# A modulation quad moved into the attention jobs, and the first expert's rows made by one-hot products

## The chip, the cores and the metric

The kernel runs on one core of one Trainium2 chip. The metric is the device time of one launch in microseconds (us), the median of several runs. The core has TensorE (PE; its weight loads are listed apart, as PEld), VectorE (DVE), ScalarE (ACT), GpSimd (POOL) and SyncE (SP), each with an instruction stream of its own; semaphores order them. DMA transfers move data between device memory and the on-chip memory, on 16 DMA engines. Matmul results go to eight PSUM banks of 128 x 512 f32.

## The reference

A block of two layers works on 256 latent and 256 context tokens of width 1024. What the change touches:

```
for l in range(DEPTH):                                  # DEPTH = 2
    mod = silu(c) @ ada_w[l] + ada_b[l]                 # 6 vectors of 1024, for latent and context tokens each
    p = modulate(rms_norm(x, norm1_g[l]), mod[0], mod[1]) @ w_in[l]       # 1952 columns
    m = four mixers of p (pooling, windowed attention, gated MLP, latent attention)
    x = x + mod[2] * (m @ w_out[l])
    h = modulate(rms_norm(x, norm2_g[l]), mod[3], mod[4])
    x = x + mod[5] * grouped_moe(h, router_w, ...)      # 16 experts, 2 chosen for a token
out = rms_norm(x_latent, final_g)
```

`grouped_moe` sums, over the two chosen experts of a token, `gate * (silu(h @ w_gate[e]) * (h @ w_up[e])) @ w_down[e]`. In the last layer only the latent tokens go on.

## The kernel before

**Weights.** All weights are streamed by SyncE through a ring of six buffers of 1 MB (`raw`), in an order written out by hand (`ORDER`, line 398); a buffer is refilled when its block is used up (`free_slot`, line 620). Each weight block of a projection or an expert is split into a high part (ScalarE, `w_hi`) and a rest (VectorE, `w_lo`), and each product is three reduced-precision matmuls. In the experts the blocks of gate and up weights go in two roles of 512 input rows each (role 0, role 1), the down weights are role 2: 3 MB for an expert.

**Modulation.** The products with `ada_w` come in twelve quads of four blocks; quads 0 to 5 belong to layer 0, 6 to 11 to layer 1. A quad is eight portions (`modulate_rows`, line 1409), in plain f32 matmuls of 32 columns; its last portion releases all four buffers (`ada_mm`). VectorE then copies the result (`take_rows`), TensorE turns it (`turn`), VectorE adds the bias (`take_modulation`). Quads 0 and 1 run at the start, 2 to 6 behind blocks 2 to 6 of the layer's input projection (`AFTER_BLOCK`), 7 behind the scores of attention job 1 (`IN_ATTENTION`), 8 in portions among the transposes of the second norm and behind the first row numbers (`IN_NORM`), 9 and 10 between the layers, 11 in layer 1's attention.

**Start.** `norm(0)` squares x, sums it by matmuls, and makes chunk by chunk nx (VectorE), nh and h_hi (ScalarE) and h_lo (VectorE). On ScalarE the splits of the first two `w_in` blocks stand before chunk 0; on VectorE the first stands behind the second nx.

**Attention of layer 0.** 16 jobs in a software pipeline: TensorE makes scores, turns the probabilities of two jobs before, multiplies by the values of three jobs before; ScalarE and VectorE do the softmax and copies, and split the first two `w_out` blocks in eight parts.

**Layer 0's experts.** The normed rows lie on chip (`h_full`) and are stored to device memory, twice: in halves (`h_half`) and whole (`h_rows`). For each expert a one-hot matrix (`onehot`, from GpSimd, the first two pairs from VectorE) multiplied by `row_of` gives row numbers (`row_numbers`); by them GpSimd's indirect DMA gathers up to 128 rows (`gather`), expert 0 and 1 by halves from `h_half`, all others from `h_rows`. TensorE transposes the rows (`tokens`), ScalarE and VectorE split them (`tokens_in`), then come role 0, role 1, and two steps later the down products. The results are scattered to `y_rows` by another indirect DMA (`scatter`). Every engine walks through the same `step(i, j, e)`. After the last scatter `next_layer` (line 743) reads the rows back into `y_back`: the lower choice of all four tiles of tokens in one transfer, then the upper choice tile by tile; VectorE and GpSimd add them in eight units, TensorE transposes, VectorE adds to x (`combine`).

## Time and profile before

| | us |
|---|---|
| median of 3 runs | 840.49 |
| the runs | 835.63, 840.49, 848.07 |
| the profiled execution, its own time | 838.9 |
| its span, first to last instruction | 837.1 |
| TensorE busy in the span | 758.3 (91%) |
| VectorE, ScalarE, GpSimd busy | 522.3, 470.7, 193.9 |
| mean granted TensorE clock | 0.953 |
| bytes moved by DMA | 202.15 MB |

The profiled execution goes roughly like this: start to 40 us, input projection of layer 0 to 171, attention to 226, output projection to 273, second norm and routing to 297, experts of layer 0 to 481, between the layers to 514, input projection of layer 1 to 588, attention, output projection and norm to 666, experts of layer 1 to the end. Busy times of TensorE have modelled ends; a wait is put down to what came last. The granted clock is given as a share of 2.4 GHz.

### The profile page before, as it was taken

Reading aid. Unit: us, or ns where it says so; the run is one execution under the profiler, and the core shown is the slowest. Engines: PE = TensorE matmul, PEld = TensorE weight load, DVE = VectorE, ACT = ScalarE, POOL = GpSimd, SP = SyncE. Lnnn points to the kernel's source line nnn. Section 1 sums busy time; section 2 is a strip of 40 time slices with the busy share of each in tenths; the row PEclk is TensorE's granted clock in tenths of the full one; section 3 lists DMA queues with packets and bytes.
Section 4 is the critical chain, followed back from the end, with each engine's and each line's share of the span. In section 5 each row is a group of like instructions: output and inputs, shape, how many; then the busy total and the mean of one; then the engine's idle time right before and its main releaser. Section 6 shows DMA issues by size and latency. Waiting matters only on the chain.

```text
span 837.1 us, 13053 instructions
## 1 busy us (share of the span) xinstructions
PE 758.3 (91%) x4850; PEld 598.7 (72%) x4850; DVE 522.3 (62%) x770; ACT 470.7 (56%) x664; POOL 193.9 (23%) x186
## 2 busy tenths in 40 slices
PE   4699899999999857999999769999999799999995
PEld 3378767856787546888888536998569588888883
DVE  2353423359632736888889556652684779988984
ACT  3454221278712626888888537631773567777763
POOL 0004000630004045799942150303102000000000
PEclk9899999999999678999999979999999699999998
DMA  9994787862211298999999889941524049999942
GB/s 362 352 261 132 273 323 267 311 218 85 67 51 51 83 346 312 331 380 359 353 361 356 306 311 289 307 152 51 180 102 153 36 151 350 350 347 351 345 167 78
DMA packets 89472, 202.15 MB, mean 241 GB/s; under 512 B 19474, under 2 KB 45628, under 8 KB 89404
## 3 DMA queue, kind: packets, MB, share of 16 engines
q1 hardware_dynamic: 83856, 191.46, 64.3%
q0 software_dynamic: 4640, 8.40, 2.7%
q10 hardware_dynamic: 908, 1.42, 0.5%
q8 instruction: 39, 0.64, 0.3%
q14 instruction: 29, 0.24, 0.1%
HBM read 196.00 MB, written 13.63 MB: 250 GB/s over the span
## 4 chain that ended last, share of the span: by engine, by line
PE 71%; DMA 8%; DVE 7%; ACT 6%; issue 5%; POOL 2%; SPq 0%; DVEq 0%; ACTq 0%; POOLq 0%
PE bank L1388 14%; PE bank L1390 14%; PE bank L1389 13%; PE bank L1415 4%; DMA y_rows<-y_sb,idx_row 3%; PE bank L1553 2%; PE bank L1700 2%; PE bank L1554 2%; PE bank L1555 2%; PE bank L1726 2%; PE bank L1712 2%; DVE w_lo L2400 2%; POOL onehot L890 1%; DMA y_back<-y_rows 1%; DMA raw<-in_w_in 1%
## 5 line engine op out<-in xcount | busy, mean ns | idle before, releaser
L2400 DVE TENSOR_TENSOR w_lo<-raw,w_hi 128x2048 fp32r<-128x2048 f32 x96 | 220.0, 2295 | 17.6 <-ACT w_hi L1250 16.7
L1250 ACT ACTIVATE w_hi<-raw 128x2048 fp32r<-128x2048 f32 x96 | 184.1, 1919 | 34.4 <-PE bank L1390 34.1
L1388 PE MATMUL bank<-h_hi,w_hi 128*128 128x512 f32 (+2 forms) x288 | 103.6, 360 | 7.8 <-DVE h_lo L2155 5.6
L1389 PE MATMUL bank<-h_lo,w_hi 128*128 128x512 f32 (+2 forms) x288 | 101.1, 351 | 0.0
L1390 PE MATMUL bank<-h_hi,w_lo 128*128 128x512 f32 (+2 forms) x288 | 101.1, 351 | 0.0
L1388 PE MATMUL bank<-w_hi,xg_hi 128*128 128x512 f32 x192 | 78.6, 410 | 2.2 <-DVE xg_lo L2568 1.7
L1390 PE MATMUL bank<-w_hi,xg_lo 128*128 128x512 f32 x192 | 76.3, 397 | 0.0
L1389 PE MATMUL bank<-w_lo,xg_hi 128*128 128x512 f32 x192 | 76.0, 396 | 0.0
L992 ACT ACTIVATE w_hi<-raw 128x2048 fp32r<-128x2048 f32 (+1 forms) x20 | 37.3, 1867 | 66.0 <-PE bank L1390 55.3
L2098 DVE TENSOR_TENSOR w_lo<-raw,w_hi 128x2048 fp32r<-128x2048 f32 (+1 forms) x20 | 45.1, 2253 | 42.3 <-ACT w_hi L992 42.1
L1388 PEld LDWEIGHTS bank<-h_hi,w_hi 128*128 128x128 f32 (+1 forms) x288 | 54.1, 188 | 17.0 <-issue 7.8
L1390 PEld LDWEIGHTS bank<-h_hi,w_lo 128*128 128x128 f32 (+1 forms) x288 | 54.1, 188 | 8.4 <-issue 0.2
L1389 PEld LDWEIGHTS bank<-h_lo,w_hi 128*128 128x128 f32 (+1 forms) x288 | 54.2, 188 | 8.0 <-issue 0.4
L1388 PE MATMUL bank<-w_hi,ht_hi 128*128 128x512 f32 x128 | 51.0, 398 | 3.5 <-ACT y_sb L1267 1.5
L1415 PE MATMUL bank<-raw,c_pad 128*32 128x256 f32 x736 | 49.4, 421 | 3.3 <-PEq L1960 3.3
L890 POOL TENSOR_SCALAR onehot<-const,slot 128x128 fp32r<-128x128 f32 x48 | 48.9, 1031 | 5.5 <-PE bank L1866 5.3
L1390 PE MATMUL bank<-w_hi,ht_lo 128*128 128x512 f32 x128 | 50.0, 391 | 0.0
L1389 PE MATMUL bank<-w_lo,ht_hi 128*128 128x512 f32 x128 | 49.9, 390 | 0.0
L879 POOL TENSOR_TENSOR nsq<-nsq 128x512 f32<-128x512 f32 (+1 forms) x12 | 16.1, 1342 | 137.7 <-ACT nsq L1023 136.7
L1553 PE MATMUL bank<-w_hi,h_hi 128*128 128x256 f32 x160 | 45.9, 287 | 0.1
L1554 PE MATMUL bank<-w_lo,h_hi 128*128 128x256 f32 x160 | 45.2, 283 | 0.0
L1555 PE MATMUL bank<-w_hi,h_lo 128*128 128x256 f32 x160 | 45.2, 283 | 0.0
(331 smaller groups left out, 1530.4 us busy)
## 6 DMA issues: line engine op xcount, KB each, us to landing
raw<-in_ada_w SPq DMA_DIRECT2D x46, 1024.0 KB, 10.7
raw<-in_moe_w_gate SPq DMA_DIRECT2D x64, 512.0 KB, 5.8
raw<-in_moe_w_up SPq DMA_DIRECT2D x64, 512.0 KB
raw<-in_moe_w_down SPq DMA_DIRECT2D x64, 512.0 KB
raw<-in_w_in SPq DMA_DIRECT2D x14, 1024.0 KB, 11.1
raw<-in_w_out SPq DMA_DIRECT2D x8, 1024.0 KB, 5.1
ada_first<-in_ada_w SPq DMA_DIRECT2D x2, 1024.0 KB, 19.3
h_half<-h_full SPq DMA_DIRECT2D x2, 1024.0 KB, 4.4
```

Source lines behind the costliest of these rows:

```text
L890: ins = pool.tensor_scalar(onehot[:, t, j * SLOTS:(j + 1) * SLOTS], const2[:, lo:lo + SLOTS], slot[:, t, e:e + 1], None, ALU.is_equal)
L992: act.activation(w_hi[slot][:, :, 0:w], raw[n % RAW][:, :, 0:w], ACT.Copy).then_inc(split_hi, 1)
L1250: act.activation(w_hi[slot][:, :, :], raw[q][:, :, :], ACT.Copy).then_inc(split_hi, 1)
L1388: pe.matmul(dst, w_hi_, x_hi_, start=first, stop=False)
L1389: pe.matmul(dst, w_hi_, x_lo_, start=False, stop=False)
L1390: return pe.matmul(dst, w_lo_, x_hi_, start=False, stop=last)
L1415: ins = pe.matmul(dst[32 * g:32 * g + 32, 0:BW], c_pad[:, k, :], wide(raw_of(l, j))[:, k % 2, g * BW:(g + 1) * BW], start=(k == 0), stop=( ...
L1553: pe.matmul(dst, h_hi[:, k, t * P:(t + 1) * P], w_hi[s][:, k, :], start=(k == 0), stop=False)
L1554: pe.matmul(dst, h_hi[:, k, t * P:(t + 1) * P], w_lo[s][:, k, :], start=False, stop=False)
L1555: ins = pe.matmul(dst, h_lo[:, k, t * P:(t + 1) * P], w_hi[s][:, k, :], start=False, stop=(k == KC - 1))
L2098: dve.tensor_tensor(w_lo[slot][:, :, 0:w], raw[n % RAW][:, :, 0:w], w_hi[slot][:, :, 0:w].bitcast(F32), ALU.subtract).then_inc(split_lo, 1)
L2400: dve.tensor_tensor(w_lo[slot][:, :, :], raw[q][:, :, :], w_hi[slot][:, :, :].bitcast(F32), ALU.subtract).then_inc(split_lo, 1)
```

## The change

Six edits go together. (1) Quad 6 leaves the place behind block 6 of the projection and takes quad 7's at attention job 1; quad 7 is done in eight portions behind jobs 4 to 11 and turned at job 12. The load order follows: `w_in` 7 before quad 6, two `w_out` blocks before quad 7. (2) At the start half of quad 1 is done ahead of a wait, and on ScalarE and VectorE chunk 0 goes ahead of the second block's split. (3) Expert 0's rows are no longer gathered: TensorE multiplies the one-hot matrix, as plain f32, with `h_full` by halves (`first_rows`), ScalarE copies the result to `x_row[0]`. (4) The stores to `h_half` are gone; expert 1's rows are gathered whole from `h_rows`. (5) The last two portions of quad 8 stand behind the rows of expert 1, its copy and addition on VectorE behind the split of expert 1's first block, its turn behind role 1 of expert 0; VectorE's one-hot matrix for the second pair has a buffer of its own. (6) `y_back`'s lower rows are read for tiles 0 and 1 first, and for tiles 2 and 3 after the upper rows of tile 1.

```diff
 norm_row = nc.alloc_sbuf_tensor_at("norm_row", [P, 2, BW], F32, offset=h_at + 4 * KC * T + 8 * D)
+onehot_b = nc.alloc_sbuf_tensor_at("onehot_b", [P, 4, 2 * SLOTS], F32R, offset=h_at + 4 * KC * T + 8 * D + 8 * BW)
...
 OUT_SLOT = [0, 1, 2, 1]
-AFTER_BLOCK = [{2: 2, 3: 3, 4: 4, 5: 5, 6: 6}, {}]
-IN_ATTENTION = [7, 11]
+AFTER_BLOCK = [{2: 2, 3: 3, 4: 4, 5: 5}, {}]
+IN_ATTENTION = [6, 11]
+BY_JOBS, BY_JOBS_FROM = 7, 4
 IN_NORM, NORM_BANK = 8, 5
...
-order = order + quad(IN_ATTENTION[l]) + w_out_blocks
-ORDER.append(order if l else order + quad(IN_NORM))
+order = order + quad(IN_ATTENTION[l])
+if l == 0:
+    order = order + w_out_blocks[:2] + quad(BY_JOBS) + w_out_blocks[2:] + quad(IN_NORM)
+else:
+    order = order + w_out_blocks
+ORDER.append(order)
...
 sp.wait_ge(q_ta, l * KC + 4 * (half + 1))
-sp.dma_start(h_half[half].rearrange("(t p) d -> p t d", p=P), h_full[:, :, cs]).then_inc((h_first, h_second)[half], 16)
 sp.dma_start(h_rows.rearrange("(t p) d -> p t d", p=P)[:, :, cs], h_full[:, :, cs]).then_inc(h_out, 16)
...
 sp.wait_ge(q_out[1], 16 * (E // 2) * k - 16)
-sp.dma_start(y_back[:, :, 0, :], rows[:, :, 0, :]).then_inc(q_lower, 16)
+sp.dma_start(y_back[:, 0:2, 0, :], rows[:, 0:2, 0, :]).then_inc(q_lower, 16)
 sp.wait_ge(q_out[1], 16 * (E // 2) * k)
 for t in range(4):
+    if t == 2:
+        sp.dma_start(y_back[:, 2:4, 0, :], rows[:, 2:4, 0, :]).then_inc(q_back[2], 16)
     sp.dma_start(y_back[:, t, 1, :], rows[:, t, 1, :]).then_inc(q_back[t], 16)
...
-def gather(k, e, half=None):
-    if half is None:
-        pool.wait_ge(h_out, 32)
-    else:
-        pool.wait_ge((h_first, h_second)[half], 16)
+def gather(k, e):
+    pool.wait_ge(h_out, 32)
     pool.wait_ge(i_row, k * (E // 2) + e // 2 + 1)
...
         pool.wait_ge(g_lo, k * E + e - 1)
-    cs = slice(0, D) if half is None else slice(half * 512, (half + 1) * 512)
-    pool.indirect_dma_start(x_row[e % 2][:, cs], None, h_rows if half is None else h_half[half], bass.IndirectOffsetOnAxis(ap=idx_row[:, e, 0:1], axis=0),
-                            bounds_check=T - 1, oob_is_err=False).then_inc(x_first if (half, e) == (0, 0) else x_in[e % 2], 16)
+    pool.indirect_dma_start(x_row[e % 2][:, :], None, h_rows, bass.IndirectOffsetOnAxis(ap=idx_row[:, e, 0:1], axis=0),
+                            bounds_check=T - 1, oob_is_err=False).then_inc(x_in[e % 2], 16)
...
     gather(k, 0)
-    gather(k, 1)
-else:
-    for half in range(2):
-        gather(0, 0, half)
-        gather(0, 1, half)
+gather(k, 1)
 for i in range(E // 2 + 2):
...
-            pool.wait_ge(q_back[t], 16 * (l + 1))
+            pool.wait_ge(q_back[t], (32 if t == 2 else 16) * (l + 1))
         if (t, half) != (0, 0):
...
 pool.wait_ge(used, done(l, N_ADA + N_WIN + N_WOUT - 1))
-pool.memset(x_row[0][:, :], 0.0)
 then(pool.memset(x_row[1][:, :], 0.0))
...
 if i == 0:
-    for r in range(HL - 1):
-        split(l, N_ADA + r)
+    split(l, N_ADA)
 if which == 1:
...
     split(l, N_ADA + HL - 1)
+if i == 0 and k == 1:
+    split(l, N_ADA + 1)
 act.wait_ge(n_x, i * KC + k + 1)
...
+def first_rows(half):
+    act.wait_ge(x_first_mm, half + 1)
+    act.activation(x_row[0][:, half * 512:(half + 1) * 512], bank[6 + half][:, :], ACT.Copy).then_inc(x_first, 1)
 def tokens_in(i, j, half=None):
...
 else:
+    first_rows(0)
     tokens_in(0, 0, 0)
     act.activation(col[:, 45:46], eps, ACT.Silu)
+    first_rows(1)
     tokens_in(0, 0, 1)
...
     ins.then_inc(n_sum, 1)
+    for k in range(4):
+        modulate_rows(1, bank[START_BANK[1]], k)
     pe.wait_ge(n_fold, 1)
...
 if i == 0:
-    modulate(1, bank[START_BANK[1]])
+    for k in range(4, KC):
+        modulate_rows(1, bank[START_BANK[1]], k)
     turn(1, bank[START_BANK[1]])
...
     turn(IN_ATTENTION[l], bank[7])
+if l == 0 and BY_JOBS_FROM <= i < BY_JOBS_FROM + KC:
+    pe.wait_ge(s_mod, BY_JOBS)
+    modulate_rows(BY_JOBS, bank[7], i - BY_JOBS_FROM)
+if l == 0 and i == BY_JOBS_FROM + KC:
+    turn(BY_JOBS, bank[7])
 if i == n_jobs:
     pe.wait_ge(s_pool, l + 1)
-    pe.wait_ge(s_mod, IN_ATTENTION[l] + 1)
+    pe.wait_ge(s_mod, (IN_ATTENTION[l] if l else BY_JOBS) + 1)
     pe.wait_ge(t_ex, 2 * (j0 + n_jobs - 1))
...
+def first_rows(half):
+    pe.wait_ge(q_p, 1)
+    for t in range(nt):
+        ins = pe.matmul(bank[6 + half][:, :], onehot[:, t, 0:SLOTS].bitcast(F32), h_full[:, t, half * 512:(half + 1) * 512],
+                        start=(t == 0), stop=(t == nt - 1))
+    ins.then_inc(x_first_mm, 1)
 def row_numbers(i, dst):
+    source = onehot_b if k == 0 and isinstance(i, int) and i == 1 else onehot
     pe.wait_ge(q_p, i + (m * (E // 2) + 1))
...
         for t in range(nt):
-            ins = pe.matmul(dst[:, 4 * j:4 * j + 4], onehot[:, t, j * SLOTS:(j + 1) * SLOTS],
+            ins = pe.matmul(dst[:, 4 * j:4 * j + 4], source[:, t, j * SLOTS:(j + 1) * SLOTS],
                             row_of[:, t, bass.ds(2 * i + j, 1), :].rearrange("p a n -> p (a n)"),
...
-    if half == 0:
-        pe.wait_ge(x_first, 16)
+    if half is not None:
+        pe.wait_ge(x_first, half + 1)
     else:
-        pe.wait_ge(x_in[j % 2], 16 * (i + j // 2) + 16 * (m * (E // 2) + 1 + j % 2))
+        pe.wait_ge(x_in[j % 2], 16 * (i + j // 2) + 16 * (m * (E // 2) + j % 2))
     for b in range(2) if half is None else (half,):
...
                 if k == 0:
+                    modulate_rows(IN_NORM, bank[NORM_BANK], KC - 2)
+                    modulate_rows(IN_NORM, bank[NORM_BANK], KC - 1)
                     pe.wait_ge(x_hi, 1)
...
             ins.then_inc(used, 1)
+    if k == 0 and e == 0:
+        turn(IN_NORM, bank[NORM_BANK])
     if j == 0 and (e is None or e < E - 4):
...
     pe.wait_ge(q_ta, KC)
+    first_rows(0)
 row_numbers(0, bank[0])
-if k == 0:
-    modulate_rows(IN_NORM, bank[NORM_BANK], KC - 2)
-    modulate_rows(IN_NORM, bank[NORM_BANK], KC - 1)
-row_numbers(1, bank[2])
+if k:
+    row_numbers(1, bank[2])
 pe.wait_ge(i_row, m * (E // 2) + 1)
...
 if k == 0:
-    turn(IN_NORM, bank[NORM_BANK])
+    first_rows(1)
+    row_numbers(1, bank[2])
 steps(pe, step, 2, k, at_end, 4)
...
 dve.tensor_tensor(nx[:, k % 2, 0:width], x_t[:, k, 0:width], bank[7][:, 0:width], ALU.mult).then_inc(n_x, 1)
-if i == 0 and k == 1:
+if i == 0 and k == 0:
     split(0, N_ADA)
-if k:
+    low(0)
+if k > (i == 0):
     low(k - 1)
...
     take_modulation(IN_ATTENTION[l], bank[7])
+if l == 0 and i == BY_JOBS_FROM + KC:
+    take_rows(BY_JOBS, bank[7])
+if l == 0 and i == BY_JOBS_FROM + KC + 1:
+    take_modulation(BY_JOBS, bank[7])
 if i < n_jobs:
...
 e = 2 * pair + j
-ins = dve.tensor_tensor(onehot[:, 0:nt, j * SLOTS:(j + 1) * SLOTS],
+ins = dve.tensor_tensor((onehot, onehot_b)[pair][:, 0:nt, j * SLOTS:(j + 1) * SLOTS],
                         const2[:, C2_IOTA:C2_IOTA + SLOTS][:, None, :].to_broadcast([P, nt, SLOTS]),
...
 if l < DEPTH - 1:
+    one_hot(1)
     row_numbers(0, 0, bank[0])
-    one_hot(1)
-    take_rows(IN_NORM, bank[NORM_BANK])
 else:
...
     split_expert(l, k, 0, i, j + 1)
+if k == 0 and e == 0:
+    take_rows(IN_NORM, bank[NORM_BANK])
+    take_modulation(IN_NORM, bank[NORM_BANK])
 if e == E - 1:
...
     split_expert(l, k, 1, 0, 0)
-row_numbers(k, 1, bank[2])
+if k:
+    row_numbers(k, 1, bank[2])
 tokens_in(0, 0, None if k else 0)
 if k == 0:
-    take_modulation(IN_NORM, bank[NORM_BANK])
+    row_numbers(0, 1, bank[2])
     further_rounds_and_rows()
```

## Rows read from the trace of the kernel before

**Rows 1.** Windows: busy (instructions) of PE, PEld, DVE, ACT, POOL; granted clock, DMA share, GB/s.

```profile
36.00:172.00 136.00, 129.40 (x941) 101.42 (x942) 52.27 (x73) 45.92 (x66) 27.29 (x33) 0.97 0.78 266
184.70:196.00 11.30, 10.74 (x101) 7.37 (x100) 10.30 (x30) 10.32 (x31) 0.00 (x0) 1.00 0.49 191
196.00:208.00 12.00, 12.00 (x79) 7.18 (x78) 11.51 (x27) 11.02 (x27) 0.00 (x0) 1.00 0.28 91
324.00:327.00 3.00, 3.00 (x10) 2.42 (x9) 1.85 (x3) 1.09 (x2) 3.00 (x5) 0.50 1.01 401
330.00:333.00 3.00, 3.00 (x15) 2.48 (x14) 1.92 (x1) 2.25 (x3) 0.00 (x0) 1.00 0.17 66
363.00:383.00 20.00, 19.37 (x100) 16.10 (x99) 17.23 (x17) 15.99 (x19) 18.89 (x13) 1.00 1.01 399
```

**Rows 2.** Timelines of the start: start us, duration us, instruction [idle before, releaser].

```profile
36.28 1.48 ACT L992 ACTIVATE w_hi<-raw 128x1536 fp32r<-128x1536 f32 x1 [0.65 <-POOL raw L793]
37.67 1.08 ACT L1094 ACTIVATE nh<-nx,mod,amp 128x256 f32<-128x256 f32 x2
38.77 0.63 ACT L1097 ACTIVATE h_hi<-nh 128x512 fp32r<-128x512 f32 x1
...
35.25 1.29 DVE L2160 TENSOR_TENSOR nx<-x_t,bank 128x512 f32<-128x512 f32 x2
36.45 2.28 DVE L2098 TENSOR_TENSOR w_lo<-raw,w_hi 128x2048 fp32r<-128x2048 f32 x1
...
40.27 0.77 PE L1388 MATMUL bank<-h_hi,w_hi 128*128 128x512 f32 x1 [5.61 <-DVE h_lo L2155]
```

**Rows 3.** Timeline of TensorE in the attention of layer 0.

```profile
174.05 3.66 PE L1415 MATMUL bank<-raw,c_pad 128*32 128x256 f32 x64
...
197.71 1.98 PE L1700 MATMUL bank<-k_mla,q_mla 96*128 96x512 f32 x4
```

**Rows 4.** Timelines of TensorE, ScalarE, VectorE from the row numbers to expert 1.

```profile
295.03 1.05 PE L1866 MATMUL bank<-row_of,onehot 128*128 128x4 f32 x8
...
305.48 1.09 PE L1879 MATMUL bank<-const,x_row 128*128 128x128 f32 x4 [6.82 <-DMA x_row<-h_half,idx_row]
...
312.30 1.48 PE L1879 MATMUL bank<-const,x_row 128*128 128x128 f32 x12
314.41 0.47 PE L1388 MATMUL bank<-w_hi,xg_hi 128*128 128x512 f32 x1 [0.63 <-DVE xg_lo L2568]
...
317.23 0.95 PE L1866 MATMUL bank<-row_of,onehot 128*128 128x4 f32 x8
...
322.59 1.94 PE L1879 MATMUL bank<-const,x_row 128*128 128x128 f32 x8 [2.61 <-DMA x_row<-h_rows,idx_row]
324.18 0.77 PE L1388 MATMUL bank<-w_hi,xg_hi 128*128 128x512 f32 x1
...
314.85 1.92 ACT L1250 ACTIVATE w_hi<-raw 128x2048 fp32r<-128x2048 f32 x1
...
316.80 2.29 DVE L2400 TENSOR_TENSOR w_lo<-raw,w_hi 128x2048 fp32r<-128x2048 f32 x1 [0.52 <-ACT w_hi L1250]
```

**Rows 5.** Load issues: w_out (size, median landing), and L708's gate halves from 297 us.

```profile
raw<-in_w_out SPq DMA_DIRECT2D x8, 1024.0 KB, 5.1
...
L708 SPq DMA_DIRECT2D raw<-in_moe_w_gate x2: 345/834/1322, 297.1 to 298.8; - x2
...
DMA to landing us min/median/max: 10.4/10.4/10.4
```

**Rows 6.** y_back: issue of lower, chain of waits, GpSimd's sums, issues of tiles 2 and 3.

```profile
481.30 0.37 SPq L762 DMA_DIRECT2D y_back<-y_rows  x1
...
484.93 9.07 DMA y_back<-y_rows
...
494.14 9.19 POOL L957 TENSOR_TENSOR y_back<-y_back 128x512 f32<-128x512 f32 x7 [7.73 <-DMA y_back<-y_rows]
...
L765 SPq DMA_DIRECT2D y_back<-y_rows x2: 441/442/443, 485.8 to 486.3; - x2
...
DMA to landing us min/median/max: 10.7/11.1/11.5
```

More of the change, by code:

```diff
@@ L270, in build @@
         h_rows = nc.dram_tensor("h_rows", (T, D), F32, kind="Internal").ap()
-        h_half = [nc.dram_tensor(f"h_half{i}", (T, 512), F32, kind="Internal").ap() for i in range(2)]
         y_rows = nc.dram_tensor("y_rows", (2 * T, D), F32, kind="Internal").ap()
@@ L340, in build @@
         x_in = [sem("x_in_even"), sem("x_in_odd")]
-        h_first, h_second, x_first, x_first_hi, x_first_lo = (sem(n) for n in ("h_first", "h_second", "x_first", "x_first_hi", "x_first_lo"))
+        x_first_mm, x_first, x_first_hi, x_first_lo = (sem(n) for n in ("x_first_mm", "x_first", "x_first_hi", "x_first_lo"))
         q_lower = sem("q_lower")
```

## The prediction

> **What bounds the kernel now.** I read the windows of busy time first, then the timelines of single engines where the diff touches them, then the landings of transfers. One engine never carries the whole span, so each edit is judged in its own stage. In the input projection of layer 0 TensorE is busy 129.4 of 136 us at a clock of 0.97 [rows 1]: what leaves TensorE there is saved. In the attention jobs 4 to 11, between 184.7 and 208 us, TensorE is busy 22.74 of 23.3 us [rows 1]: the reader should see that it is as full there, so that work put there is paid for. At the start TensorE waits 5.61 us for the first h_lo [rows 2]. At the first expert it waits 6.82 us for the gathered rows of expert 0, and 2.61 us again for those of expert 2, just ahead of expert 1's products [rows 4]. Between the layers everything waits for y_back [rows 6]. In the steady experts the DMA engines show a share of 1.01 and 399 GB/s, TensorE is busy 19.37 and GpSimd 18.89 of 20 us [rows 1]: three resources are nearly full at once, so a delay at their start is not made up later.
>
> **The modulation quad.** A quad on TensorE costs 3.6 us (64 instructions, 3.66 with its modelled end) [rows 3]. Quad 6 leaves the projection (minus 3.6) and takes quad 7's place at job 1 (no change). Quad 7 is cut into eight portions of 8 instructions, 0.45 us each, behind jobs 4 to 11: 3.6 us. The idle time that could take them in is 11.30 minus 10.74, 0.56 us, in one stretch and 12.00 minus 12.00, none, in the other [rows 1]. Sum: minus 3.6 plus 3.6 minus 0.56, a gain of 0.6 us. Bounds: nothing gained, and 3.6 us if the portions fill gaps that modelled ends hide; I take the low side because two full windows are the nearest rows. VectorE gets quad 7's copy and additions (under 1 us) at jobs 12 and 13, where TensorE leads; cost nothing, 1 us if that cover is gone. The load queue: w_in 7, w_out 0 and 1 are issued earlier, quad 7 when quad 6 is used up at job 1; four loads behind each other at 5.1 us for the first [rows 5] and 2.6 for each further one (1.05 MB at 399 GB/s [rows 1]) are in by 13 us, while the last portion pair wants its block more than 20 us on. Quad 8 then waits for quad 7's last portion, at about 208 us, but is wanted only in the transposes of the second norm, behind the whole output projection: covered.
>
> **The start.** ScalarE now makes nh and h_hi of chunk 0 before it splits the second block (1.48 us), and VectorE does the first w_lo after one nx, not two. ScalarE is free at 36.28 minus 0.65, 35.63 us; nh 1.08 and h_hi 0.63 are done by 37.4. VectorE: nx to 35.9, w_lo 2.28 to 38.2, then h_lo, which with its signal took 0.87 (from 39.40, where h_hi ended, to 40.27): 39.0 instead of 40.27 [rows 2], a gain of 1.3 us. It passes on, since TensorE bounds what follows. The halving of quad 1 brings modulation forward by up to half of 3.6 us, but w_lo, which waits for the landed block, is then last; I count nothing. Bounds: 0 and 1.6 us.
>
> **The first expert.** Before: row numbers at 295.03, rows transposed at 305.48, role 1 of expert 0 finished at 317.23, expert 1's products at 324.18 [rows 4]. After, step by step, at full clock, since TensorE now has work: one-hot products, 4 matmuls of 128x512 plain f32. None runs here with these operands; scores of the same form cost 1.98 us for two [rows 3], so 0.95 each and 3.8 per half (bounds 3.6 and, at half clock, 7.6; I take 3.8, as 295.03 is at full clock). 295.0 + 3.8 = 298.8; row numbers 1.0: 299.8; transposes 0.5: 300.3; second half 3.8: 304.1; row numbers 1.0: 305.1; twelve products 2.8 (314.41 to 317.23 [rows 4]): 307.9; twelve transposes 1.5 [rows 4]: 309.4; two portions of quad 8, 1.0: 310.4; role 1 of expert 0: 313.2, against 317.23. Here the change leads by 4.0 us.
>
> But the step that was moved also releases loads. Quad 8 holds four of the six load buffers until its last portion, and expert 1's first weights were issued at 297.1, right behind it [rows 5]. Now that is 310.4, 13 us later. What waits for that is a queue: expert 1's block lands after 5.1 us at 315.5 (bounds: the 5.1 of a w_out load and the 10.4 that this very load took behind full queues [rows 5]; nearer to 5.1, as the h_half copy is gone, the h_rows copy is done and only gathers share the engines); ScalarE 1.9 to 317.4; VectorE 2.3 to 319.7 [rows 4]; only behind that in VectorE's order come the copy of quad 8 (0.4), and with it TensorE's turn (0.5), which stands before the row numbers (1.0): 321.6. Then hid_m turned and the rows of expert 2, 1.9 us with the clock down again (1.94 in [rows 4]): expert 1's products at 324.0, against 324.18. So 0.2 us is left of 4.0. The clock costs about the same as before: expert 1's first products ran at a granted 0.50, the 1.2 GHz level [rows 1], after TensorE's waits of this stage, and it stands still for some 7 us now too, only later. Bounds for the head: plus 4.0 if the block is not last, minus 5.1 if it lands after 10.4. The gather of expert 1 has 304 to 309 us to land and is not on the path; of GpSimd's four gathers three are gone, and the one-hot of pair 1 on VectorE now stands before a wait: no cost.
>
> The rule on a transfer's cost can be set beside this. The Trainium skill, "DMA: Bandwidth & Descriptors", section "Anatomy of one DMA", gives a fixed part of about 2.0 us, mostly the write's receipt, plus the bytes at 436 GB/s, by which the block would land after 4.4 us (an estimate). The trace's 5.1 is slower and decides; by the page the head would gain 0.9 us. The same page, section "Queues, rings and completion order", speaks against the change: each DMA engine goes round the queues that have work. The gather of expert 2 is issued at about the same time as the block, and half of the bytes moved would be its own; an estimate from the page is 1.2 us more (0.5 MB at 436 GB/s), by which the head would lose 1.0 us. No run here shows the two alone.
>
> **The rows back, by pairs of tiles.** The lower rows (2 MB) were issued at 481.30, the upper rows of tile 0 at 484.93, which landed 9.07 us later; tiles 2 and 3, issued 485.8 and 486.3, landed 10.7 and 11.5 later, at 496.5 and 497.8 [rows 6]. That is 1.3 us per 0.5 MB: they land one behind the other, so 1 MB less ahead of tile 0 is 2.6 us. Tiles 2 and 3 have the same bytes ahead. GpSimd's seven sums (9.19 us, 1.3 each [rows 6]) now begin at 491.5 instead of 494.14, reach tile 2 behind the third, at 495.5, wait to 496.5 and end at 501.7 instead of 503.33. I take 1.5 us, with 0.1 for the pause between the first 1 MB and the next issue. Bounds: 0, if another transfer were last, and the full 2.6.
>
> **Sum.** 0.6 + 1.3 + 0.2 + 1.5 = 3.6 us. The profiled execution took 838.9 us (span 837.1 and 1.8 around it), 1.6 below the median of 840.49 (three runs); 838.9 - 3.6 = 835.3, and from the median 836.9. I say 836.
>
> **Rivals.**
> 1. The late weights decide, and it ends slower. Place: the first block of expert 1. For it: 13 us less lead for a queue that runs at a share of 1.01 afterwards [rows 1]. Against it: the share was only 0.17 at 330 to 333 us [rows 1], so the loads had been ahead of the buffers, and 1 MB of stores is gone. It decides from a landing of 5.1 + 3.6 = 8.7 us on. At 10.4 the head loses 5.1, and the whole is 1.7 slower; with another 2 us of half clock 3.7: 842 to 844. Chance 0.2.
> 2. Spreading does hide the quad, and the head keeps part of its lead: 3.6 instead of 0.6, plus 1 to 3 us. For it: TensorE's ends are modelled. Against it: no idle row in 12 us. 829 to 833. Chance 0.15.
> 3. The change does little: VectorE's w_lo or the landing block sets the start, and y_back's other tiles set the sums. 838 to 841. Chance 0.2.
> 4. The forecast, 833 to 838: chance 0.45.
>
> The rivals reach from 829 to 844. Leaving out a tenth at each side, and with runs of one kernel from 835.63 to 848.07, the range is 829 to 843. Two per cent is 17 us (about what a measurement of this kernel can tell from no change); the sum of all upper bounds, 1.6 + 3.6 + 4.0 + 2.6 = 11.8 us, does not reach it, nor does the lower one. Faster by over 2%: 0.03; within: 0.94; slower: 0.03.
>
> **What would show it.** Right: the projection's TensorE time down by 3.6 us and the jobs' up by 3; first product near 39.0; role 1 of expert 0 done near 313 and then 7 us of idle TensorE at the low clock until expert 1's w_lo; first sum of y_back 2 to 3 us sooner after its issue. Wrong: jobs 4 to 11 no longer than before, expert 1's products before 322 or after 327, or a wait for a weight load inside the steady experts.

## The result: 0.8% slower

| | before | after |
|---|---|---|
| median, us (20 runs each, taken together) | 841.14 | 847.35 |
| range of the runs, us | 835.63 to 848.07 | 841.34 to 852.64 |
| profiled execution, us | 838.9 | 850.8 |
| its span, us | 837.1 | 849.0 |
| mean granted TensorE clock | 0.953 | 0.942 |
| TensorE busy, us | 758.3 | 771.7 |

The ratio is 1.0076, with a 95% interval of 1.0056 to 1.0096: within 2%, but 6.2 us slower where 3.6 us of gain were forecast, and outside the range. Ratios and intervals, here and below, leave out the few executions in a slower state of the chip (one of the kernel with the rows back alone, at 1269 us, and a few of the kernel before). The two profiled executions differ by 11.9 us, since that of before lay 2.2 us under its median and that of after 3.5 over; so a loss read from these two traces is an upper one until other profiles bear it out.

**The profile after.** Windows of the changed kernel, with the columns of [rows 1]:

```profile
36.00:172.00 136.00, 127.47 (x860) 101.90 (x860) 52.29 (x70) 43.13 (x61) 24.86 (x32) 0.92 0.68 231
156.00:160.00 4.00, 3.11 (x14) 3.11 (x15) 3.22 (x2) 0.98 (x1) 3.92 (x2) 0.53 0.49 145
160.00:164.00 4.00, 4.00 (x25) 4.00 (x23) 0.00 (x0) 0.00 (x0) 3.76 (x4) 0.62 0.35 121
191.24:209.00 17.76, 17.76 (x154) 9.67 (x153) 14.85 (x38) 13.48 (x37) 0.00 (x0) 1.00 0.31 110
363.00:383.00 20.00, 19.47 (x100) 16.19 (x99) 17.21 (x17) 16.07 (x19) 18.88 (x13) 1.00 0.99 386
```

The projection's clock was 0.97 [rows 1] and is 0.92. The low parts have two places: up to 47 us, where the kernel before was at full clock from 45 us, and from 156 to 163 us, where it never fell. The portions stand in 17.76 us without any idle time. The steady experts are as before. Now chosen lines of the timelines (start, duration, instruction, idle time before it and what ended it). First the start and the end of the projection:

```profile
35.80 3.37 POOL L799 COPY raw<-raw 128x64 f32<-128x64 f32 x4 [34.50 <-DMA raw<-in_w_in]
35.97 2.29 DVE L2124 TENSOR_TENSOR w_lo<-raw,w_hi 128x2048 fp32r<-128x2048 f32 x1 [1.52 <-ACT w_hi L989]
39.05 0.76 PE L1393 MATMUL bank<-h_hi,w_hi 128*128 128x512 f32 x1 [5.87 <-DVE h_lo L2181]
39.26 1.48 ACT L989 ACTIVATE w_hi<-raw 128x1536 fp32r<-128x1536 f32 x1 [1.68 <-POOL raw L799]
40.78 1.76 DVE L2124 TENSOR_TENSOR w_lo<-raw,w_hi 128x1536 fp32r<-128x1536 f32 x1 [1.28 <-ACT w_hi L989]
42.59 0.80 PE L1393 MATMUL bank<-h_hi,w_hi 128*128 128x512 f32 x1 [0.65 <-DVE w_lo L2124]
...
152.31 1.08 PE L1573 MATMUL bank<-kv_low,w_ukv 128*64 128x512 f32 x4
152.41 1.91 ACT L989 ACTIVATE w_hi<-raw 128x2048 fp32r<-128x2048 f32 x1 [14.67 <-PE bank L1395]
154.36 2.48 DVE L2124 TENSOR_TENSOR w_lo<-raw,w_hi 128x2048 fp32r<-128x2048 f32 x1 [0.58 <-ACT w_hi L989]
156.89 0.58 PE L1561 MATMUL bank<-w_hi,h_hi 128*128 128x256 f32 x1 [3.50 <-DVE w_lo L2124]
```

The first product comes at 39.05, as forecast, against 40.27 [rows 2]. But GpSimd's four small copies, which swap columns of the second block, now take 3.37 us, and the second block's split is late by that. At 152.4 the reader sees the loss that the prediction did not have: ScalarE and VectorE split block 7 only now, when block 6 is finished, and TensorE waits 3.50 us for it, after the products of up_k (`kv_low` by `w_ukv`). Before, quad 6 stood in exactly this place:

```profile
151.15 3.66 PE L1415 MATMUL bank<-raw,c_pad 128*32 128x256 f32 x64
151.30 1.91 ACT L992 ACTIVATE w_hi<-raw 128x2048 fp32r<-128x2048 f32 x1 [14.72 <-PE bank L1390]
153.25 2.43 DVE L2098 TENSOR_TENSOR w_lo<-raw,w_hi 128x2048 fp32r<-128x2048 f32 x1 [0.64 <-ACT w_hi L992]
154.74 1.08 PE L1565 MATMUL bank<-kv_low,w_ukv 128*64 128x512 f32 x4
155.75 0.38 PE L1553 MATMUL bank<-w_hi,h_hi 128*128 128x256 f32 x1
```

The split ended at 155.68, and block 7's first product began at 155.75: there was no slack left, so whatever left TensorE here had to come back as a wait. The head of the experts with SyncE's first load (SPq), answering to [rows 4, 5]:

```profile
301.50 3.67 PE L1878 MATMUL bank<-h_full,onehot 128*128 128x512 f32 x8
304.60 1.35 PE L1888 MATMUL bank<-row_of,onehot 128*128 128x4 f32 x8
...
313.86 1.47 PE L1901 MATMUL bank<-const,x_row 128*128 128x128 f32 x12
315.27 1.07 PE L1420 MATMUL bank<-raw,c_pad 128*32 128x256 f32 x16
316.61 0.35 SPq L713 DMA_DIRECT2D raw<-in_moe_w_gate  x1
323.33 1.91 ACT L1248 ACTIVATE w_hi<-raw 128x2048 fp32r<-128x2048 f32 x1 [6.81 <-issue]
325.27 2.29 DVE L2431 TENSOR_TENSOR w_lo<-raw,w_hi 128x2048 fp32r<-128x2048 f32 x1 [7.43 <-ACT w_hi L1248]
327.48 0.42 DVE L2146 COPY norm_row<-bank 128x256 f32<-128x256 f32 x1
327.95 0.69 PE L1435 MATMUL bank<-const,norm_row 128*128 128x128 f32 x2 [8.63 <-DVE norm_row L2146]
330.48 1.95 PE L1901 MATMUL bank<-const,x_row 128*128 128x128 f32 x8
```

This is the queue that the prediction described: last portions of quad 8, issue, landing, split, copy of quad 8, turn. Only from the block's first issue to the start of its split 6.7 us pass (316.61 to 323.33), not 5.1; in four other profiles with the same order (quad undone, split 7 early, first expert only, one piece) it is 5.8 to 6.5. Between the layers (answering to [rows 6]):

```profile
488.70 0.37 SPq L766 DMA_DIRECT2D y_back<-y_rows  x1
493.00 2.83 POOL L799 COPY raw<-raw 128x64 f32<-128x64 f32 x4 [5.11 <-issue]
495.91 1.48 ACT L989 ACTIVATE w_hi<-raw 128x1536 fp32r<-128x1536 f32 x1 [2.76 <-POOL raw L799]
496.29 1.27 POOL L955 TENSOR_TENSOR y_back<-y_back 128x512 f32<-128x512 f32 x1 [0.46 <-DMA y_back<-y_rows]
497.43 1.76 DVE L2124 TENSOR_TENSOR w_lo<-raw,w_hi 128x1536 fp32r<-128x1536 f32 x1 [1.87 <-ACT w_hi L989]
499.10 0.42 DVE L2146 COPY gap_row<-bank 128x256 f32<-128x256 f32 x1
499.57 0.69 PE L1435 MATMUL bank<-const,gap_row 128*128 128x128 f32 x2 [4.79 <-DVE gap_row L2146]
500.57 1.50 DVE L2219 TENSOR_TENSOR y_back<-y_back 128x512 f32<-128x512 f32 x1
```

GpSimd's first sum starts 7.6 us behind the issue of the lower rows, where it was 12.8 (481.30 to 494.14 [rows 6]): the rows are back sooner. VectorE's first sum, which TensorE needs first, starts 11.9 behind it, hardly sooner than 12.8: VectorE is busy with the second block and with quad 9.

### The profile page after: what moved, and what is told of

It is laid out like the page before. It is cut to its first block, busy times and chain, and to the rows that moved or that the text cites. A ratio compares the mean times of both kernels' runs of the same rounds, so it can differ in the third digit from the quotient of the medians.

```text
span 849.0 us, 13080 instructions
## 1 busy us (share of the span) xinstructions
PE 771.7 (91%) x4866; PEld 605.1 (71%) x4866; DVE 524.9 (62%) x770; ACT 471.7 (56%) x666; POOL 194.3 (23%) x182
## 4 chain that ended last, share of the span: by engine, by line
PE 70%; POOL 8%; DVE 6%; ACT 6%; issue 5%; DMA 4%; SPq 0%; POOLq 0%; ACTq 0%; DVEq 0%
PE bank L1393 13%; PE bank L1395 12%; PE bank L1394 12%; PE bank L1420 5%; POOL onehot L896 4%; PE bank L1561 3%; PE bank L1562 2%; PE bank L1563 2%; POOL x_row L906 2%; PE bank L1708 2%; PE bank L1734 2%; PE bank L1720 2%; DVE w_lo L2431 2%; DMA raw<-in_w_in 2%; ACT w_hi L1248 1%
## 5 line engine op out<-in xcount | busy, mean ns | idle before, releaser
L1561 PE MATMUL bank<-w_hi,h_hi 128*128 128x256 f32 x160 | 47.9, 299 | 3.6 <-DVE w_lo L2124 3.5
L1562 PE MATMUL bank<-w_lo,h_hi 128*128 128x256 f32 x160 | 47.2, 295 | 0.0
L1563 PE MATMUL bank<-w_hi,h_lo 128*128 128x256 f32 x160 | 47.1, 294 | 0.0
```

The lines of the kernel that those rows point to most:

```text
L1561: pe.matmul(dst, h_hi[:, k, t * P:(t + 1) * P], w_hi[s][:, k, :], start=(k == 0), stop=False)
L1562: pe.matmul(dst, h_hi[:, k, t * P:(t + 1) * P], w_lo[s][:, k, :], start=False, stop=False)
L1563: ins = pe.matmul(dst, h_lo[:, k, t * P:(t + 1) * P], w_hi[s][:, k, :], start=False, stop=(k == KC - 1))
```

## Stage by stage, in this and other profiles

Each length is the difference of two starts in a profile's timelines (a quad by its first product; "rows back" is from the issue of the lower rows to the first product of quad 10). The first product is given by its own start; the attention jobs end at the first product of the output projection. The kernels of the later columns are described below.

| us | before | after | quad only | quad undone | split 7 early | first expert only | loads early | all cures | all cures, no quad |
|---|---|---|---|---|---|---|---|---|---|
| first product | 40.27 | 39.05 | 42.26 | 38.95 | 38.59 | 39.99 | 42.18 | 38.76 | 38.73 |
| to quad 2 | 36.16 | 38.27 | 36.21 | 36.64 | 38.86 | 36.53 | 36.50 | 35.83 | 35.39 |
| quad 5 to first scores | 37.00 | 39.47 | 39.06 | 36.99 | 33.20 | 36.99 | 36.99 | 33.20 | 37.00 |
| attention jobs | 55.19 | 59.48 | 59.48 | 55.18 | 59.49 | 55.19 | 55.18 | 59.48 | 55.19 |
| row numbers (first rows) to expert 1's products | 29.15 | 30.58 | 27.89 | 29.51 | 30.14 | 30.06 | 25.86 | 25.48 | 25.65 |
| rows back | 27.58 | 30.87 | 26.93 | 31.31 | 24.92 | 27.33 | 25.75 | 24.96 | 23.21 |
| quad 11 to the end | 245.3 | 245.6 | 245.7 | 249.2 | 248.5 | 248.7 | 245.6 | 249.5 | 245.3 |

The attention jobs repeat to 0.1 us in kernels with the same code there, and so does quad 5 to the first scores where TensorE does not wait (37.0 and 33.2). Where it waits for block 7 the wait is 3.50 us each time, but the stretch is 39.47, 39.06 and, with the quad in one piece, 38.27, as the clock came back at 163.1, 163.0 and 160.8 us. Of the 11.9 us between the profiles of before and after, 6.8 lie in the two rows of the quad, 3.3 in the rows back, 1.4 at the first expert and 0.9 ahead of quad 2.

The last row is 245 or 249 us for a stage in which nothing was changed. The clock makes the difference: in all 18 profiles of the study TensorE has the same waits there (to 0.3 us), up to 75 us behind quad 11, and the granted clock falls to 0.50; in seven it was back 77 to 79 us behind quad 11 (245.2 to 245.7 us in all), in eleven only after 84 to 88 us (248.5 to 249.5). Both lengths occur with and without each of the edits, so they are put down to none.

## The experiments

Times are medians; the ratio is to the kernel before, run beside them (its medians were 839.74 to 841.23). It is estimated from the runs and not the quotient of two medians; the two can differ by 0.2%. First each edit alone.

**The quad alone.** Edit (1) of the change on the kernel before:

```diff
-        AFTER_BLOCK = [{2: 2, 3: 3, 4: 4, 5: 5, 6: 6}, {}]
-        IN_ATTENTION = [7, 11]
+        AFTER_BLOCK = [{2: 2, 3: 3, 4: 4, 5: 5}, {}]
+        IN_ATTENTION = [6, 11]
+        BY_JOBS, BY_JOBS_FROM = 7, 4
...
```

> The kernel before with the first edit alone: quad 6 at job 1, quad 7 in eight portions behind jobs 4 to 11, the load order with it. Theory 1 (cover lost): the quad behind block 6 hid the split of block 7; without it TensorE waits about 3.5 us for VectorE's w_lo of block 7, block 7 then runs some 2.5 us longer at the low clock, and each portion costs 0.57 us instead of 0.45: -3.6 + 3.5 + 2.5 + 4.3 = 5 to 7 us slower than the kernel before, ratio 1.006 to 1.008. Theory 2 (the head costs it): within 1.5 us of before, and no wait ahead of block 7 over 1 us. Theory 3 (a drift of the clock that belongs to no edit): each edit alone is within 1.5 us.

846.93 us (six runs), ratio 1.0103 (1.0064 to 1.0143); block 7 waited 3.50 us and the jobs took 59.48 us. Theory 1 holds, theories 2 and 3 fall: this edit alone costs as much as the whole change. The ratio lies above the 1.006 to 1.008 expected, and its interval reaches down to them; the two stages account for 6.4 us.

**The start alone.**

```diff
-                    for r in range(HL - 1):
-                        split(l, N_ADA + r)
+                    split(l, N_ADA)
...
+                    if i == 0 and k == 1:
+                        split(l, N_ADA + 1)
...
```

> The kernel before with the edits of the start alone. Theory 1: the first product comes 1.2 us earlier, but GpSimd's four swap copies of the second block take 3.4 us beside VectorE's w_lo instead of 0.8, so that TensorE waits for the second block and about 0 to 1 us more is spent by 46 us: within 1 us of before, 0 to +1. Theory 2 (head) and theory 3 (drift): the forecast stands here, 1.3 us faster.

838.5 us, ratio 0.9997 (0.9974 to 1.0021): no difference. Its first product came at 38.74, and the four copies took 3.29 us.

**The first expert alone.**

```diff
+                        first_rows(0)
                     row_numbers(0, bank[0])
...
+                                        modulate_rows(IN_NORM, bank[NORM_BANK], KC - 2)
+                                        modulate_rows(IN_NORM, bank[NORM_BANK], KC - 1)
...
```

> The kernel before with the edits of the first expert alone (first_rows, quad 8's last portions and turn behind expert 0's products, no h_half). Theory 1: the lead to role 1 of expert 0 is there and is given back at expert 1's first weights: 0.3 to 1.5 us slower. Theory 2 (the head costs it): 5 us or more slower, with the weights of expert 1 landing late and the low clock held past 340 us. Theory 3: within 1.5 us.

842.75 us, ratio 1.0041 (1.0016 to 1.0065): the second loss. The median lies 3.0 us above that of before, where I expected 0.3 to 1.5; the interval, 1.3 to 5.5 us, touches that. The expectation came from two traces, and the profile of before was itself slow here: 29.15 us to expert 1's products, where the profiles of the quad alone, the start alone and the rows back alone, with the same code, show 27.89, 28.32 and 27.73. Its own 30.06 is 2.1 more than the mean of these.

**The rows back alone.**

```diff
-                    sp.dma_start(y_back[:, :, 0, :], rows[:, :, 0, :]).then_inc(q_lower, 16)
+                    sp.dma_start(y_back[:, 0:2, 0, :], rows[:, 0:2, 0, :]).then_inc(q_lower, 16)
...
```

> The kernel before with y_back's lower rows by pairs of tiles alone. Theory 1: the first sums start about 2.5 us sooner after the issue, GpSimd's last one 1.5 us sooner: 0.5 to 2.5 us faster. Rival: quad 9's chain (its products, the split of the second block, its rows on VectorE) was equally late and VectorE's first sum does not move: within 0.5 us of before, and only GpSimd's sums are earlier. Theory 3: within 1.5 us.

841.12 us, ratio 1.0013 (0.9984 to 1.0042). In its profile the rows came back 3.7 us sooner than before (23.86 us from issue to quad 10 instead of 27.58), yet the timed runs show nothing. In the same profile the last stage took 249.0 us where before had 245.3, the clock's difference of the table, so the profile as a whole is no shorter either. What the edit is worth stayed open; see below.

Next the two causes, each undone in one place.

**Block 7 split early, all else as changed.** By the first theory it is not the quad's place that matters but the split behind it.

```diff
-        SPLIT_AFTER = [{1: (3,)}, ...
-        SPLIT_FIRST = [{3: 4, 4: 5, 5: 6, 6: 7}, {}]
+        SPLIT_AFTER = [{1: (3,), 5: (7,)}, ...
+        SPLIT_FIRST = [{3: 4, 4: 5, 5: 6}, {}]
```

> The changed kernel, but ScalarE and VectorE split block 7 of w_in at the end of their step 5 and not behind block 6. Theory 1 (cover lost): what the quad behind block 6 covered was this split; with the split moved ahead, TensorE goes from up_k to block 7 without the 3.5 us wait and without the low clock behind it: from quad 5 to the first scores 33.4 to 34 us instead of 39.5, the jobs still 59.5, the whole 5 to 6 us faster than the changed kernel, 841 to 843 us, ratio to before 1.000 to 1.003. Rival: the two splits in a row delay VectorE's own steps of blocks 5 and 6, and TensorE waits there instead: 38 to 40 us, ratio 1.006 or more.

840.93 us, ratio 1.0005 (0.9974 to 1.0037), 6.4 us below the changed kernel's median. VectorE's timeline and then TensorE's, of this kernel:

```profile
145.30 2.29 DVE L2124 TENSOR_TENSOR w_lo<-raw,w_hi 128x2048 fp32r<-128x2048 f32 x1
...
152.48 1.08 PE L1573 MATMUL bank<-kv_low,w_ukv 128*64 128x512 f32 x4
153.49 0.39 PE L1561 MATMUL bank<-w_hi,h_hi 128*128 128x256 f32 x1
153.72 0.28 PE L1562 MATMUL bank<-w_lo,h_hi 128*128 128x256 f32 x1
153.83 0.29 PE L1563 MATMUL bank<-w_hi,h_lo 128*128 128x256 f32 x1
```

Block 7 follows up_k at once, at full clock (0.12 us from product to product; in the changed kernel, at the low clock, 0.21). Quad 5 to first scores is 33.20, 3.8 below before: now the projection does save its 3.6 us. This theory is shown.

**The quad back in its place, the rest as changed** (the first diff reversed).

> The changed kernel with its first edit undone: quad 6 behind block 6 again, quad 7 at job 1. Theory 1 (the quad costs most): 6 to 8 us faster than the changed kernel, 839 to 841.5 us, ratio to before 0.999 to 1.003; quad 5 to first scores 37.0, the jobs 55.2. Rival (the head and what follows the experts costs it): 845 us or more, ratio 1.005 or more.

844.47 us, ratio 1.0035 (1.0000 to 1.0070). The stages went back as foreseen (36.99 and 55.18), 6.8 us in all, but the whole gained 2.9 us only, less than expected: neither theory's figure, and the interval overlaps that of the changed kernel. What is left would be the other three edits' loss, of which the first expert's 1.0041 is one part; the profile also shows 31.31 us in "rows back", 3.7 more than before.

**The loads early**, on the first-expert edit alone: its last two portions of quad 8 stand ahead of the first transposes.

```diff
-                                        modulate_rows(IN_NORM, bank[NORM_BANK], KC - 2)
-                                        modulate_rows(IN_NORM, bank[NORM_BANK], KC - 1)
...
                     if k:
                         row_numbers(1, bank[2])
+                    else:
+                        modulate_rows(IN_NORM, bank[NORM_BANK], KC - 2)
+                        modulate_rows(IN_NORM, bank[NORM_BANK], KC - 1)
```

> The kernel before with the edits of the first expert, but the last two portions of quad 8 kept ahead of the first transposes, so that its four buffers are free some 9 us sooner. Theory 1 (late weights): expert 1's first block is issued about 5 us behind the first one-hot product instead of 15, is in before ScalarE asks for it, and the rows of expert 2 are transposed 23 to 25 us behind the first one-hot product instead of 28.5: 4 to 5 us faster than with all edits of the first expert, 837 to 839 us, ratio to before 0.996 to 0.999. Rival (the DMA engines are full at any rate, or GpSimd's gather of expert 2 is as late): 27 us or more, 841 to 843 us, ratio 1.003 to 1.005.

840.01 us, ratio 0.9979 (0.9950 to 1.0008), as expected, and the interval lies clear below that of the same edit without it (1.0016 to 1.0065). By the medians it is 2.7 us, less than the 4 to 5 expected; to expert 1's products it took 25.86 us instead of 30.06. TensorE's waits from the one-hot products to expert 1 (waited for: us in total, times, longest), first without, then with the early loads:

```profile
PE bank L1427 <- DVE norm_row L2130: 8.1, 1, 8.1
PE bank L1885 <- DVE gate_slot L2429: 0.3, 1, 0.3
```

```profile
PE bank L1885 <- DMA x_row<-h_rows,idx_row: 2.2, 1, 2.2
PE bank L1427 <- DVE norm_row L2131: 1.4, 1, 1.4
```

The 8.1 us ahead of the turn are 1.4, and the next wait in line shows up, 2.2 us for the gather of expert 1, which had been hidden.

**Quad 7 in one piece**, on the changed kernel.

```diff
-                    if l == 0 and BY_JOBS_FROM <= i < BY_JOBS_FROM + KC:
+                    if l == 0 and i == BY_JOBS_FROM + KC - 1:
                         pe.wait_ge(s_mod, BY_JOBS)
-                        modulate_rows(BY_JOBS, bank[7], i - BY_JOBS_FROM)
+                        modulate(BY_JOBS, bank[7])
```

> The changed kernel, with quad 7 in one piece behind job 11 instead of eight portions behind jobs 4 to 11; its place in the load order and the turn at job 12 stay. Theory 1: a portion costs 0.45 us of products and 0.12 of changing over, so the jobs take 58.6 to 58.8 us instead of 59.5. Rival (it is the jobs that are crowded, not the change between forms): 59.3 or more.

One execution only, 853.75 us, above every one of the changed kernel's 20, so no time can be read from it; by its profile the jobs took 58.89 us instead of 59.48, where 58.6 to 58.8 were expected. TensorE's timeline of the changed kernel shows what a portion costs, 0.57 us to the next start for eight products that fill 0.45 within a whole quad (3.6 us for 64, [rows 3]):

```profile
191.24 0.64 PE L1420 MATMUL bank<-raw,c_pad 128*32 128x256 f32 x8
191.81 0.70 PE L1697 MATMUL bank<-k_na,q_na 64*128 64x256 f32 x4
```

So the quad's 3.6 us are paid in full, 3.7 over before, and cutting it in eight costs another 0.6.

**Both cures together.**

> The changed kernel with both cures: block 7 split in step 5, and the last two portions of quad 8 ahead of the first transposes. Theory (two separate losses, one at block 7, one at expert 1's first weights): they add, 5 to 6 and 4 to 5 us off the changed kernel: 836 to 838.5 us, ratio to before 0.994 to 0.998. Rival (what is won at the experts is given back behind them, between the layers): 840 us or more, no better than the first cure alone.

839.15 us, ratio 0.9969 (0.9937 to 1.0001). They add less than foreseen, and the median lies just outside of what I expected. Beside the profile of split 7 early, the way to expert 1's products is 3.2 us shorter (26.92 for 30.14) and the rows back are 2.4 longer (27.31 for 24.92), which is what the rival said; in one GpSimd's copies between the layers took 2.10 us, in the other 0.76. The start, 38.76 us to quad 2 with a pause at 42 us, is as slow in both: neither cure touches it.

**The swap on ScalarE.** At the start GpSimd's four copies took 0.76 us in the profile of before, 3.37 in that of after. (Between the layers they took 2.83 in both, from 483.58 us in that of before, so that trace already held the slow case.) The copies read `raw` while VectorE's w_lo reads `raw` and `w_hi`.

```diff
                 if r == N_ADA + 1:
+                    rk = raw[n % RAW]
+                    for half in range(2):
+                        for part in range(2):
+                            to, fr = 160 + 16 * part + 8 * half, 128 + 16 * part + 8 * (1 - half)
+                            last = act.activation(rk[:, :, to:to + 8], rk[:, :, fr:fr + 8], ACT.Copy)
+                    last.then_inc(s_swap, 1)
                     act.wait_ge(s_swap, l + 1)
...
```

GpSimd's own `swap` and its two calls go.

> The same, and the four small copies that swap columns of block 1 of w_in go from GpSimd to ScalarE, in both layers. Theory (a shared path): on GpSimd they take 0.76 us where VectorE's w_lo starts behind them and 2.8 to 3.4 where it starts beside them; on ScalarE they take 0.8 to 1.0 always. From ScalarE's first w_hi to its second 3 us at most, no products waiting for w_lo of block 1 at 42 us, and the products of quad 9's rows back 2 us sooner between the layers: 1.5 to 3 us faster than both cures alone, 833.5 to 836.5 us. Rival (something else ended those waits): within 0.8 us.

833.2 us (six runs), ratio 0.9899 (0.9850 to 0.9947): 6 us below the median of both cures, more than expected, though the intervals still touch (0.9937 to 1.0001 there). It is the lowest median of the study, 1.0% below the kernel before and 14 us below the changed one. Its timelines at the start, then its window from 42 us, then the windows of the changed kernel there:

```profile
37.23 0.68 ACT L968 ACTIVATE raw<-raw 128x64 f32<-128x64 f32 x4
37.94 1.49 ACT L982 ACTIVATE w_hi<-raw 128x1536 fp32r<-128x1536 f32 x1
38.76 0.77 PE L1386 MATMUL bank<-h_hi,w_hi 128*128 128x512 f32 x1 [5.84 <-DVE h_lo L2175]
39.46 1.76 DVE L2118 TENSOR_TENSOR w_lo<-raw,w_hi 128x1536 fp32r<-128x1536 f32 x1 [0.26 <-ACT w_hi L982]
```

```profile
42.00:44.00 2.00, 2.00 (x9) 1.43 (x8) 1.37 (x3) 1.97 (x4) 0.00 (x0) 0.84 1.03 412
```

```profile
42.00:44.00 2.00, 1.41 (x3) 1.06 (x4) 2.00 (x4) 1.22 (x3) 0.00 (x0) 0.50 1.02 412
44.00:46.00 2.00, 2.00 (x6) 1.38 (x5) 1.38 (x3) 1.94 (x5) 0.00 (x0) 0.50 1.03 412
```

The pause is gone, the granted clock is 0.84 where it was 0.50 (the 1.2 GHz level), and quad 2 follows after 35.83 us instead of 38.27. (The line from 42 to 44 us of the changed kernel holds its pause of 0.65 us.)

**The same without the quad's move.**

> The kernel before with the edits of the start, of the first expert with its cure, of the rows back, and the swap on ScalarE; quads 6 and 7 where they were. Theory: with its cover mended the move of the quad is worth nothing by itself (33.2 + 59.5 us for 37.0 + 55.2 of projection and jobs): within 1.5 us of the same kernel with the quad moved. Rival: the move helps by 3 us or more once block 7 is split early, or still costs 3.

834.59 us, ratio 0.9927 (0.9895 to 0.9959): within 1.4 us of the kernel with the move. With its cover mended, the move is worth nothing that can be told.

**The kernel before with the swap alone.**

> The kernel before with the swap on ScalarE alone. Theory: the first product comes at 40.3 to 40.9 us in every profile, where the profiles with the swap on GpSimd had it at 40.0 to 40.3 or, where w_lo ran beside it, at 42.2 to 42.8: 0.5 to 2.5 us faster than before at the median, ratio 0.997 to 0.9995. Rival: ScalarE was the busier engine there and loses the 0.8 us: 0 to 1 us slower.

836.85 us, ratio 0.9954 (0.9926 to 0.9982), 4.2 us below the median of before and beyond what I expected. The first product came at 39.97. The swap was the kernel's own fault, not the change's. Profiles with it on GpSimd and the old start show 40.27 and 39.99 with copies of 0.76 to 0.78 us, but 42.18, 42.26 and 42.83 with copies of 2.88 to 2.91, and quad 2 at 76.4 to 78.7 us, where it comes at 75.7 and 76.0 with the swap on ScalarE. That is some 2 us of the 4.2; where the rest is won was not traced.

Then four runs on what was open, each taking one edit out of (or, the last, one thing into) the cured kernels, 834.59 and 833.2 us.

**Without the rows back by pairs.**

```diff
-                    sp.dma_start(y_back[:, 0:2, 0, :], rows[:, 0:2, 0, :]).then_inc(q_lower, 16)
+                    sp.dma_start(y_back[:, :, 0, :], rows[:, :, 0, :]).then_inc(q_lower, 16)
```

> The kernel with the start, the cured first expert and the swap on ScalarE (cures_swap_no_quad: 834.6 us), with the lower rows of y_back in one transfer again. Theory: with quad 9's chain out of the way the first sums are what TensorE waits for, and they come 2.6 us later: from quad 9 to quad 10 26.5 to 27.5 us instead of 23.4, 2 to 4 us slower, 836.5 to 838.5. Rival: something else is as late; within 1 us.

836.45 us, ratio 0.9945 (0.9917 to 0.9972), 1.9 us slower at the median, less than the two intervals can tell apart.

**Without the first-expert edit** (its diff reversed).

> The same kernel (cures_swap_no_quad), with the first expert as before and the start, the rows back and the swap kept. Theory: with its late weights cured, the edit brings expert 1's products from 28.3 to 25.6 us behind the row numbers, of which 1 us or so is lost by the next pair: 1 to 2.5 us slower without it, 835.5 to 837. Rival: GpSimd and the DMA engines bound what follows at any rate: within 0.7 us.

836.01 us, ratio 0.9948 (0.9922 to 0.9974), 1.4 us slower at the median.

**Without the start edit** (its diff reversed).

> The same kernel (cures_swap_no_quad), with the start as before. Theory: first product 40.0 instead of 38.7 us, and 0.4 us less lost behind it: 1 to 1.5 us slower without it, 835.5 to 836. Rival: the clock rises with the first products wherever they begin, or w_lo of block 1 is last: within 0.5 us.

836.1 us, ratio 0.9948 (0.9923 to 0.9974), 1.5 us slower at the median; first product at 40.10.

**The quad moved, in one piece, all cures** (the diff of the one piece, on the fastest kernel).

> The kernel with all cures and the quad moved (cures_swap: 833.2 us), quad 7 in one piece behind job 11. Theory: the jobs take 58.9 us instead of 59.5: 0.6 us faster, not to be told from none by the timed runs, but by the length of the stage. Rival: the long piece starves ScalarE and VectorE, and mix waits: the stage is as long or longer.

835.56 us, ratio 0.9935 (0.9909 to 0.9960). The jobs took 58.88 us, as in the other profile with one piece, and the timed runs do not show the 0.6 us: the median is 2.4 above the 833.2, with intervals that overlap. So once the swap is off GpSimd, each of the three other edits stands at 1.4 to 1.9 us of gain by the medians. All have the same sign, and none can be told from nothing by the intervals.

## Why the prediction was wrong, by its own steps

- **"Quad 6 leaves the projection (minus 3.6)": this step failed.** It costed the removal as pure gain and never asked what the quad had covered; [rows 1] showed TensorE busy 129.4 of 136 us, and I took that for a stage in which nothing else could be last. Behind block 6 the split of block 7 takes 1.9 and 2.5 us, and the quad lay beside it, with 0.07 us to spare. The wait is 3.50 us, so the removal gave nothing, and the low clock behind it (0.53 and 0.62 up to 164 us) makes quad 5 to scores 2.5 longer: plus 2.5 for minus 3.6. The early split shows it: without the wait the stretch is 33.20, and the kernel 6.4 us faster.
- **"8 x 0.45 us, minus 0.56": mis-sized.** The jobs took 4.29 more, not 3.0. A portion costs 0.57 from its start to the next instruction (191.24 to 191.81), 4.56 for eight, so idle time took in at most 0.3. Rival 2, hiding, is out.
- **The start, minus 1.3: right in its place, wrong as "it passes on".** The first product was at 39.05 against 39.0 forecast. The four copies were not in the sum. In this profile 2.1 us are lost up to quad 2, more than the 1.2 won. With the swap on ScalarE the profiles keep the gain, quad 2 at 74.12 with the edit and 75.97 without it; the timed 1.5 us are within the intervals.
- **The first expert, plus 4.0 minus 3.8.** The chain was right in every link: first rows 3.1 us each instead of 3.8 (and below the lower bound of 3.6: the scores that served as a row are dearer), the last portion of quad 8 done 14.8 us behind the first one-hot product where I had 15.4, then 6.7 us from issue to split instead of 5.1. From the first one-hot product to expert 1 it took 30.58 us where 29.0 were forecast. That is the 1.6 of the landing; the 0.6 won ahead of it was lost in small links behind. The Trainium skill, "DMA: Bandwidth & Descriptors", section "Anatomy of one DMA", whose formula is for transfers issued by GpSimd while these loads are SyncE's, would have the block in after 4.4 us (an estimate); the trace disagrees by 2.3. The gather that the prediction thought of stood beside it: GpSimd issued two, at 316.12 and 317.52, and the prediction's 1.2 us for one come near the 1.6; but ten further half-blocks of weights were issued by 323 us too, and no run separates them. Rival 1 put the point of decision at 8.7 us, which was not reached in the step; but its mechanism, late weights, was the second cause, since the usual length before was 28.1 (the mean of four other profiles with the old code: quad alone, start alone, rows back alone, swap alone) and not the 29.15 of one trace.
- **The rows back, minus 1.5: right for GpSimd, wrong for the path.** The first sum came 7.6 us behind the issue instead of 12.8; over all profiles of the study it was 8.2 with pairs (eleven) and 11.5 without (seven), 3.3 sooner where 2.6 were forecast. But the chain of quad 9 was next: swap, w_hi, w_lo, copy, turn, then VectorE's first sum. What was late next was not named. In the profiles with pairs where the swap took 0.76 us here (rows back alone, split 7 early) the first y_back products came 9.3 and 9.8 us behind the issue; with 2.10 us (both cures) 12.4; with 2.8 us (after, quad undone, one piece) 13.5 to 14.0, no sooner than the 13.7 of before, whose copies also took 2.83. That the copies decide this is read from those profiles. The 31 us of the whole stretch have a second cause: from the first y_back products to quad 10 it was 17.35 us in these three, all at a granted clock of 0.50, and 13.9 in before at 0.86. The prediction had no clock in this term; why it stayed low there is not shown.
- **Range.** The upper end, 843, was built from late weights alone. The quad's term had nothing as its worst case, though a removal can also uncover a wait. With nothing gained in the projection and the portions paid, its bound would have been 3.6 us lost; with the low clock and the dearer portions the stages show 6.8.

**What stays open.** The clock after the start: with a pause of 0.47 or 0.48 us near 42 us it rose at 42.1, 43.6 and 44.7 us (start alone, quad undone, one piece), with one of 0.65 us at 47.0 to 47.9 in three (after, split 7 early, both cures). Whether the length of the pause or something else decides is not settled, and neither is what decides in the last stage, where the waits are the same. The edits' medians alone (plus 7.2, minus 1.2, plus 3.0, plus 1.4) add up to 10.4, and their ratios to 1.5%, while the change as a whole costs 6.2 us or 0.8%. An estimate from the five intervals gives 0.6% of uncertainty to that difference: by the medians (0.5% apart) chance is enough, by the ratios (0.8%) not quite. Whether the edits take something from each other is not shown.

## What to carry to other kernels

Before work is taken off a full engine, look at what the other engines do during it: if their last step before the next block stands there, the work was cover, and the step has to move ahead first (here one table entry, worth 6.4 us). When a moved step also frees buffers, keep the freeing part where it was and move the rest. And take the length of a stage from more than one profile: one trace hid 1 us of the first expert's loss, and the profiles show 245 or 249 us for a stage that nobody touched, by the clock alone.
